# Two transformer layers: when results are taken, where up-projections, the last gate and the relu product stand

## The chip, the cores and the metric

One core of a Trainium2 chip. Its engines are TensorE (matmuls), VectorE, ScalarE, GpSimd and SyncE (it issues the loads); they run unsynchronised and wait for each other on semaphores. The metric is the time of one execution on the device in microseconds; the time before is 3451.94 us, the median of 3 runs (3451.68 to 3452.9).

## The reference, cut to what matters

Everything is fp32. A first model of two layers (FFN, retention or neighbourhood attention, FFN) runs on 512 rows and ends in an RMS norm; its 256 rows feed a second model of two layers, of width 1024, which is all that the change touches apart from bookkeeping. One layer of it:

```python
h = _rms_norm(x, norm_mix_pre[l])
proj = jnp.einsum('bsd,de->bse', h, w_in[l])
dq, dk, dv, mq, mk, mv, c_q, c_kv, k_pe, g = jnp.split(proj, IN_OFFSETS, axis=-1)
oa = _diff_attention(...)                 # 4 heads, two softmaxes each, then a sub-norm
ob = _moba_attention(mq, mk, mv, ...)     # 4 heads; 256 tokens are one block: causal softmax
q = jnp.einsum('bsr,re->bse', _rms_norm(c_q, mla_q_norm[l]), mla_w_uq[l])     # + rope on 32 dims
kv = jnp.einsum('bsr,re->bse', _rms_norm(c_kv, mla_kv_norm[l]), mla_w_ukv[l]) # k: 64 dims + rope(k_pe)
oc = _dense_causal_attention(q, k, v, ...)                                    # 8 heads
br = jnp.einsum('bsgc,gcd->bsgd', stack([oa, ob, oc]), w_branch[l])
gates = jax.nn.sigmoid(g.reshape(B, S, N_BRANCH, D_MODEL))
mixed = jnp.einsum('bsd,de->bse', jnp.sum(gates * br, axis=2), w_out[l])
x = x + _rms_norm(mixed, norm_mix_post[l])
h = _rms_norm(x, norm_mlp_pre[l])
u = jnp.square(jax.nn.relu(jnp.einsum('bsd,df->bsf', h, w_up[l])))            # 1024 -> 4096
x = x + _rms_norm(jnp.einsum('bsf,fd->bsd', u, w_down[l]), norm_mlp_post[l])
```

## The kernel before

**Projections.** All projections go through one list of `Gemm` objects. Each is cut into groups, a group into chunks. A usual group is one weight block of 8 K tiles of 128 by 256 columns, 1 MB, and makes two chunks of 128 output rows by 256 tokens. To keep fp32 accuracy, both operands are held as a high part and a low part in a reduced format, and each product is three matmuls (high-high, high-low, low-high): 24 matmuls a chunk, 48 a group. The branch groups have 4 K tiles, 24 matmuls. The up-projections of the latent attention are one group each: `mla_uq` 8 chunks of 6 matmuls, `mla_ukv` 8 chunks of 3 and two of 3 that are 512 wide.

**Weights.** SyncE loads block after block into six slots. ScalarE copies a block to `w_high` (L808, two pieces, three buffers), VectorE subtracts to get `w_low` (L1215, two pieces). `splits_upto(s + 1)` at the start of a group's step on these two engines splits the block two groups ahead. So each engine's order is: split a later block, then take the results (evict the chunks) of this group.

**Banks.** A chunk goes to PSUM bank n % 4; TensorE waits for chunk n - 4 to be taken. Even and odd chunks have a semaphore each. Each call of `gemm` on ScalarE and VectorE first waits until the last two chunks before it have been taken.

**Order.** TensorE, ScalarE and VectorE each walk the same program as Python generators; a `yield` ends a group. `both` chains several gemms, `alongside` puts groups of projections between the units of an attention. A unit is one softmax of 128 queries: TensorE makes the scores (L1905, plus bias L1906), VectorE the row maximum (L1411, L1412), ScalarE the exponentials (L974), VectorE a diagonal matrix of inverse sums (`dg`, L1421 with L1424 or L1427), TensorE turns the probabilities with it (L1922), ScalarE copies them (`hf`, L955), TensorE multiplies by the values (L1936), ScalarE and VectorE take the output in two parts (L963, L1436). Scores run two units ahead. In `alongside`, a lag of 1 puts ScalarE and VectorE one unit behind TensorE with each group.

**One layer, in TensorE's order.** `mla_c` (latents, first two groups "wide": both blocks, K tile by K tile, four banks), `diff_q`, `diff_k`, `diff_v`, `mla_uq`, rotation of the rope key, `mla_ukv`, rotations and `moba_q`, the differential attention with `moba_k` and `moba_v` beside it, `gate0`, the sub-norm, the block attention, the latent attention with `branch0`, `gate1`, `branch1`, `gate2` (16 groups) beside its 16 units, `branch2`, `mixed`, norm and residual, then four times `up` (4 groups) and `down` (4 groups), norm and residual. In the first layer these stand at: up-projections 2317 to 2343 us, differential attention 2359 to 2418, block attention 2439 to 2465, latent attention 2471 to 2583, branch2 2583 to 2595, mixed to 2631, the four up and down pairs from 2637 to 2843. The second layer follows 587 us later.

**Taking results.** `row_scaled` and `sigmoid` chunks multiply by the row factor of the norm (`rb`; it isn't applied to the inputs). A gate chunk is one VectorE multiply (L1327) and one ScalarE tanh (L920). A `mix` chunk is multiply (L1375), add (L1380), and for the last branch also a ScalarE high part `yh` (L938) and a VectorE low part `yl` (L1386), which `mixed` reads. A `relu2` chunk of `up` is, one after the other: VectorE max with 0 times the row factor `rb2` (L1359), VectorE square (L1362), ScalarE high part (L934), VectorE low part (L1365). `down` reads the eight chunks of `up` as its K tiles.

**Norms.** ScalarE squares the chunks (L821), TensorE sums them with ones (L1763), ScalarE takes the root (L841), VectorE the reciprocal, TensorE spreads it over the partitions (`spread`, L1778). For a "raw" norm ScalarE copies the spread row to `rb` or `rb2` (`row_out`, L869). `opened` and `joined` place these sums between the K tiles of the wide groups.

## Time and profile before

| | us |
|---|---|
| median of 3 runs | 3451.94 |
| lowest, highest | 3451.68, 3452.9 |
| the profiled execution | 3449.64 |
| span of its trace | 3447.9 |
| TensorE busy | 3236.3 (94%) |
| VectorE busy | 1879.9 (55%) |
| ScalarE busy | 1151.5 (33%) |
| mean granted TensorE clock | 0.960 |

The span runs from the first instruction to the last; 1.7 us of the execution lie around it. Matmuls are pipelined and their ends are modelled, so TensorE's 94% is not how full it is; its waits and the starts of its instructions tell more. DMA engines are busy 39% of the time for the weights.

### The profile page before, as it was taken

What the parts mean: (1) busy time and instruction counts of PE and PEld (TensorE: products, weight loads), DVE (VectorE), ACT (ScalarE), POOL (GpSimd) and SP (SyncE); (2) the same over time, 40 slices, a digit from 0 to 9 for tenths busy, and PEclk for the clock granted to TensorE, in tenths of its full rate; (3) what the DMA queues carried; (4) which work ended last, traced back from release to release, by engine and by line L of the source; (5) the groups of instructions that cost most, each with busy time, mean ns of one, the idle gap of its engine ahead of it and who ended that gap; (6) DMA issues with size and microseconds to landing.
All of it is one profiled execution on the core that took longest, in us unless ns stands there. A gap on an engine that the chain in (4) does not pass through costs nothing.

```text
span 3447.9 us, 46967 instructions
## 1 busy us (share of the span) xinstructions
PE 3236.3 (94%) x19181; PEld 2794.8 (81%) x19181; DVE 1879.9 (55%) x3739; ACT 1151.5 (33%) x1945; POOL 38.5 (1%) x74
## 2 busy tenths in 40 slices
PE   8999999999899999999999999998898998888898
PEld 4788878888678888788877779996887998778798
DVE  1777663544468966433344345555456666445665
ACT  2322232323232222322233334442444344344442
POOL 1000000000000000000000000000000000000000
PEclk9999999999999999999989999998999999899899
DMA  8445441221145656323232125652234554224352
GB/s 254 122 146 170 129 141 62 92 68 62 61 123 169 216 171 189 86 80 110 80 100 66 61 81 153 178 176 74 86 103 150 163 167 125 62 86 147 110 183 87
DMA packets 501215, 421.36 MB, mean 122 GB/s; under 512 B 9947, under 2 KB 497675, under 8 KB 501001
## 3 DMA queue, kind: packets, MB, share of 16 engines
q1 hardware_dynamic: 497976, 412.33, 38.9%
q0 software_dynamic: 3024, 6.03, 0.7%
q8 instruction: 152, 2.49, 0.3%
q14 instruction: 63, 0.51, 0.0%
HBM read 417.20 MB, written 1.12 MB: 121 GB/s over the span
## 4 chain that ended last, share of the span: by engine, by line
PE 86%; DVE 9%; ACT 3%; issue 2%; SPq 0%; DMA 0%; DVEq 0%; ACTq 0%
PE gemm L1829 71%; DVE w_low L1215 3%; PE aux L1763 2%; PE aux L1922 2%; PE aux L1905 2%; PE aux L1936 2%; ACT w_high L808 1%; PE aux L1906 1%; PE gemm L1978 1%; PE aux L2067 1%; PE aux L1797 1%; DVE hf L1362 1%; DVE xt L1257 1%; DVE yt L1359 1%; PE aux L2055 1%
## 5 line engine op out<-in xcount | busy, mean ns | idle before, releaser
L1215 DVE TENSOR_TENSOR w_low<-raw,w_high 128x1024 fp32r<-128x1024 f32 (+2 forms) x720 | 759.1, 1096 | 369.8 <-ACT w_high L808 368.7
L808 ACT ACTIVATE w_high<-raw 128x1024 fp32r<-128x1024 f32 (+2 forms) x720 | 647.9, 948 | 692.4 <-PE gemm L1829 408.3
L1829 PE MATMUL gemm<-xh,w_high 128*128 128x512 f32 (+1 forms) x1792 | 676.9, 378 | 21.1 <-DVE xl L1243 21.1
L1829 PE MATMUL gemm<-xl,w_high 128*128 128x512 f32 (+1 forms) x1792 | 667.2, 372 | 0.0
L1829 PE MATMUL gemm<-xh,w_low 128*128 128x512 f32 (+1 forms) x1792 | 666.9, 372 | 0.0
L1829 PE MATMUL gemm<-yh,w_high 128*128 128x256 f32 x1344 | 392.2, 292 | 29.0 <-DVE yl L1386 10.2
L1829 PEld LDWEIGHTS gemm<-xh,w_high 128*128 128x128 f32 x1792 | 342.0, 191 | 93.2 <-issue 18.2
L1829 PEld LDWEIGHTS gemm<-xh,w_low 128*128 128x128 f32 x1792 | 342.2, 191 | 63.1
L1829 PEld LDWEIGHTS gemm<-xl,w_high 128*128 128x128 f32 x1792 | 342.7, 191 | 60.8 <-issue 0.7
L1829 PE MATMUL gemm<-yl,w_high 128*128 128x256 f32 x1344 | 384.5, 286 | 0.0
L1829 PE MATMUL gemm<-yh,w_low 128*128 128x256 f32 x1344 | 383.7, 286 | 0.0
L1186 DVE SCALAR_TENSOR_TENSOR macc<-raw,sc,macc 128x256 f32<-128x256 f32 x728 | 301.9, 479 | 4.0
L1829 PEld LDWEIGHTS gemm<-yh,w_high 128*128 128x128 f32 x1344 | 260.2, 194 | 37.2 <-issue 18.1
L1829 PE MATMUL gemm<-hid_high,w_high 128*128 128x512 f32 (+1 forms) x704 | 262.2, 372 | 0.0
L1829 PEld LDWEIGHTS gemm<-yl,w_high 128*128 128x128 f32 x1344 | 260.5, 194 | 0.1
L1829 PEld LDWEIGHTS gemm<-yh,w_low 128*128 128x128 f32 x1344 | 260.0, 193 | 0.0
L1829 PE MATMUL gemm<-hid_low,w_high 128*128 128x512 f32 (+1 forms) x704 | 259.5, 369 | 0.0
L1829 PE MATMUL gemm<-hid_high,w_low 128*128 128x512 f32 (+1 forms) x704 | 259.1, 368 | 0.0
L1829 PE MATMUL gemm<-act_high,w_high 128*128 128x256 f32 (+1 forms) x752 | 223.7, 298 | 30.9 <-DVE act_low L1365 17.9
L1829 PE MATMUL gemm<-act_low,w_high 128*128 128x256 f32 (+1 forms) x752 | 217.7, 290 | 0.0
L1829 PE MATMUL gemm<-act_high,w_low 128*128 128x256 f32 (+1 forms) x752 | 217.2, 289 | 0.0
L1349 DVE TENSOR_TENSOR hf<-sq,gemm 128x512 f32<-128x512 f32 (+1 forms) x88 | 54.5, 620 | 284.2 <-PE gemm L1829 284.2
(303 smaller groups left out, 4414.1 us busy)
## 6 DMA issues: line engine op xcount, KB each, us to landing
raw<-in_ffn_w_in SPq DMA_DIRECT2D x176, 512.0 KB, 5.3
raw<-in_w_mod SPq DMA_DIRECT2D x72, 1024.0 KB, 7.1
raw<-in_w_in SPq DMA_DIRECT2D x50, 1024.0 KB, 5.2
raw<-in_w_up SPq DMA_DIRECT2D x32, 1024.0 KB, 5.4
raw<-in_w_down SPq DMA_DIRECT2D x32, 1024.0 KB, 5.1
raw<-in_ffn_w_out SPq DMA_DIRECT2D x32, 768.0 KB, 4.6
raw<-in_ret_w_in SPq DMA_DIRECT2D x24, 1024.0 KB, 5.2
raw<-in_ffn_w_out SPq DMA_DIRECT2D x32, 640.0 KB, 4.1
```

The source lines that it names most:

```text
L808: act.activation(wh[i % SPL][:, a:b], raw[slot_of["w", i]][:, a:b], ACT.Copy).then_inc(w_high, 1)
L1186: dve.scalar_tensor_tensor(out=acc, in0=raw[slot][:, WB * k:WB * k + WB], scalar=sc[:, k, v:v + 1], in1=acc, op0=ALU.mult, op1=ALU.add).th ...
L1215: dve.tensor_tensor(wl[slot][:, a:b], raw[slot][:, a:b], wh[i % SPL][:, a:b].bitcast(F32), ALU.subtract).then_inc(w_low, 1)
L1257: dve.scalar_tensor_tensor(out=x_t[:, (N["s0"] + k) % 4, :], in0=N["src"](c)[:, ts * T:ts * T + T], scalar=N["scale"](c, ts), in1=mean_of( ...
L1349: dve.tensor_tensor(hf[:, pr % 2, 0:tok], sa[:, pr % 2, 0:tok], ps[:, 0:tok], ALU.mult).then_inc(odd_free, 1)
L1359: dve.scalar_tensor_tensor(out=yt[:, pr % 4, :], in0=ps[:, 0:T], scalar=0.0, in1=rb_of[name][0], op0=ALU.max, op1=ALU.mult).then_inc(free( ...
L1362: dve.tensor_tensor(hf2[:, pr % 2, :], yt[:, pr % 4, :], yt[:, pr % 4, :], ALU.mult).then_inc(hid_f, 1)
L1763: ins = pe.matmul(mean_of(N)[:, o:o + w], s_q[:, i % N["sqn"], P * j:P * j + P], fsq[:, c, :] if kind == "f" else ones[:, 0:1], start=c == ...
L1829: ins = pe.matmul(out, l_, r_, start=first and j == 0, stop=last and j == 2)
L1905: pe.matmul(sc_[:, 0:k], un["qk"][0], un["qk"][1], start=True, stop=True, skip_group_check=True)
L1922: ins = pe.matmul(aux[2][:, P * kt:P * kt + P], pe_[:, uq % a.slots, P * kt:P * kt + P], dg_[:, uq % a.slots, :], start=q == 0, stop=q == ...
L1936: ins = pe.matmul(aux[3][r0:r1, 0:P], tile["v"](kt), pt_[:, tg % 2, P * kt:P * kt + P], start=kt == 0, stop=kt == nkt - 1)
```

## The change

- `alongside`: lag now counts groups. ScalarE and VectorE split and take a group when TensorE is at the next one, no longer one unit later.
- The values `diff_v` and `moba_v` become two gemms of one group each; `mla_uq` stands between the halves of `diff_v`, `mla_ukv` after the second.
- In groups of 8 or more chunks (`mla_uq`, `mla_ukv`) the split of a later block comes after the sixth chunk instead of before the first.
- The rope: the key is rotated after `mla_ukv`, its seven copies move into the first gate, the angles are made between the two groups of `diff_q`; TensorE waits for less before its rotations.
- The block attention has no group step of ScalarE and VectorE in it; both groups of the gate are taken behind it.
- `gate2` leaves the latent attention. It and `branch2` become four gemms of one group each, in turn: gate quarter, branch quarter. The mixed result goes to `ah`, `al` instead of `yh`, `yl`, and `mixed` is wide.
- `up`: ScalarE makes relu of the chunk, VectorE multiplies it with the chunk itself; high and low part of a chunk come after the next chunk's product. The row factor of this norm is no longer applied: the MLP's output is off by its square per token, and the norm behind it gets eps divided by the fourth power of the factor instead, made of one tiny operation (`joint`) with the mean square.
- The sums of squares of the last two chunks of the first norm move from K tile 7 to K tile 3 of the first projection.

```diff
@@ alongside
-                y = x - lag
-                upto = y * nb // na if not atts[name].narrow else 0 if y < 0 else 1 + y * (nb - 2) // na
-                while done < upto:
+                upto = 1 + x * (nb - 2) // na if atts[name].narrow else x * nb // na
+                while done < upto - lag:
@@ gemms
-            qkv("diff", 0, 0.125, q2, k2, v2)
+            q_and_k("diff", 0, 0.125, q2, k2)
+            v_half("diff", 0, v2, 0)
             add(f"mla_uq{l}", ...
+            v_half("diff", 0, v2, 1)
...
+            for g in range(2):
+                gate(g, f"gate{g}{l}", 0, 4)
+                branch(g, f"branch{g}{l}", 0, 4)
+            for q in range(4):
+                gate(2, f"gate2{l}{q}", q, q + 1)
+                branch(2, f"branch2{l}{q}", q, q + 1)
+            add(f"mixed{l}", "copy_y", A_groups(A["w_out_2"][l], D),
+                (lambda c: ah[:, c, :], lambda c: al[:, c, :]), L, arg=0)
@@ with_mla
-            return [f"{k}{l}" for k in ("branch0", "gate1", "branch1", "gate2")]
+            return [f"{k}{l}" for k in ("branch0", "gate1", "branch1")]
@@ scalar: gemm
-                    splits_upto(s + 1)
+                    if len(ch) < 8:
+                        splits_upto(s + 1)
...
                         elif g.kind == "relu2":
-                            pr = g.hid0 + i
-                            act.wait_ge(hid_f, g.rl0 + i + 1)
-                            act.activation(ah[:, i, :], hf2[:, pr % 2, :], ACT.Copy).then_inc(hid_high, 1)
+                            act.wait_ge(chunk_ready, n + 1)
+                            if i >= 4:
+                                wait_chunk_out(act, n - 4)
+                            act.activation(yt[:, i % 4, :], ps[:, 0:T], ACT.Relu).then_inc(relu_ready, 1)
+                            for k in ([i - 1] if i else []) + ([i] if i == g.nch - 1 else []):
+                                wait_chunk_out(act, g.n0 + k)
+                                act.activation(ah[:, k, :], hf2[:, k % 2, :], ACT.Copy).then_inc(hid_high, 1)
...
                         n += 1
+                        if ci == 5 and len(ch) >= 8:
+                            splits_upto(s + 1)
@@ vector: gemm
-                            dve.scalar_tensor_tensor(out=yt[:, pr % 4, :], in0=ps[:, 0:T], scalar=0.0, in1=rb_of[name][0],
-                                                     op0=ALU.max, op1=ALU.mult).then_inc(free(n), 1)
-                            dve.wait_ge(free(n), n // 2 + 1)
-                            dve.tensor_tensor(hf2[:, pr % 2, :], yt[:, pr % 4, :], yt[:, pr % 4, :],
-                                              ALU.mult).then_inc(hid_f, 1)
-                            dve.wait_ge(hid_high, pr + 1)
-                            dve.tensor_tensor(al[:, i, :], hf2[:, pr % 2, :], ah[:, i, :].bitcast(F32),
-                                              ALU.subtract).then_inc(hid_low, 1)
+                            dve.wait_ge(relu_ready, g.rl0 + i + 1)
...
+                            dve.tensor_tensor(hf2[:, i % 2, :], yt[:, i % 4, :], ps[:, 0:T], ALU.mult).then_inc(free(n), 1)
+                            for k in ([i - 1] if i else []) + ([i] if i == g.nch - 1 else []):
+                                dve.wait_ge(hid_high, g.hid0 + k + 1)
+                                dve.tensor_tensor(al[:, k, :], hf2[:, k % 2, :], ah[:, k, :].bitcast(F32),
+                                                  ALU.subtract).then_inc(hid_low, 1)
@@ vector: inverses
+                if N["name"][:8] == "mlp_post":
+                    dve.wait_ge(sq_used, N["sq0"] + N["nc"])
+                    dve.scalar_tensor_tensor(out=joint[:, 2:4], in0=mean_of(N)[:, 0:2], scalar=1.0 / D, in1=joint[:, 0:2],
+                                             op0=ALU.mult, op1=ALU.add).then_inc(var_ready, 1)
...
+                elif N["name"][:7] == "mlp_pre":
+                    chain(dve.tensor_tensor(joint[:, 2:4], root[:, 0:2], root[:, 0:2], ALU.mult))
+                    dve.scalar_tensor_tensor(out=joint[:, 0:2], in0=joint[:, 2:4], scalar=EPS, in1=joint[:, 2:4],
+                                             op0=ALU.mult, op1=ALU.mult).then_inc(inv_ready, 1)
@@ tensor
-                        spread(norms[pre])
+                        if pre == "mix_pre1":
+                            spread(norms[pre])
...
-                if k == DC - 1:
+                if k == 3:
                     for c in range(6, DC):
                         mean_square(norms["final"], c)
+                if k == DC - 1:
                     spread(norms["final"])
...
-                    pe.wait_ge(roped, 2 * MH * l + (MH + k - 3 if k >= 4 else 1))
+                    if k >= 3:
+                        pe.wait_ge(roped, 2 * MH * l + (1 if k == 3 else k - 2))
...
-                pe.wait_ge(o_low, atts[f"mla{l}"].t1)
-                run(gemm(f"branch2{l}"))
-                run(gemm(f"mixed{l}", lambda kc: pe.wait_ge(mix_low, 8 * l + kc + 1)))
+                for q in range(4):
+                    run(gemm(f"gate2{l}{q}"))
+                    pe.wait_ge(o_low, atts[f"mla{l}"].t1)
+                    run(gemm(f"branch2{l}{q}"))
+                run(gemm(f"mixed{l}", lambda kc: pe.wait_ge(mix_low, 8 * l + kc + 1), wide=True))
```

## Rows read from the trace of the kernel before

**Rows 1.** The page, part 4: shares of the chain that ended last.
```profile
PE 86%; DVE 9%; ACT 3%; issue 2%; SPq 0%; DMA 0%; DVEq 0%; ACTq 0%
```

**Rows 2.** TensorE's waits, 2262 to the end: waited for, us in total, times, longest.
```profile
PE aux L1922 <- DVE dg L1427: 21.0, 7, 4.6
PE gemm L1829 <- DVE act_low L1365: 17.9, 12, 4.0
...
PE aux L1922 <- DVE dg L1424: 11.2, 8, 3.2
PE aux L1922 <- ACT hf L955: 10.9, 6, 3.2
PE gemm L1829 <- DVE yl L1386: 10.2, 5, 4.0
...
PE gemm L1829 <- DVE w_low L1215: 5.9, 2, 3.0
...
PE aux L1778 <- DVE r_columns L1232: 1.7, 1, 1.7
```

**Rows 3.** Windows: us, busy of PE, PEld, DVE, ACT, POOL (count), granted clock, DMA share, GB/s.
```profile
2317.00:2343.00 26.00, 16.97 (x90) 13.47 (x88) 16.00 (x36) 9.67 (x17) 0.00 (x0) 0.80 0.31 93
...
2359.00:2418.00 59.00, 48.26 (x279) 39.19 (x279) 21.50 (x75) 15.72 (x51) 0.00 (x0) 0.86 0.17 54
...
2439.00:2470.00 31.00, 24.56 (x170) 22.42 (x169) 15.10 (x55) 13.08 (x43) 0.00 (x0) 0.94 0.14 44
...
2700.00:2747.00 47.00, 45.82 (x386) 45.52 (x386) 31.48 (x48) 18.98 (x24) 0.00 (x0) 1.00 0.56 180
...
2905.00:2925.00 20.00, 14.70 (x87) 11.40 (x85) 12.67 (x27) 9.19 (x15) 0.00 (x0) 0.90 0.43 127
...
2941.00:3005.00 64.00, 53.61 (x279) 43.50 (x280) 21.42 (x74) 16.16 (x52) 0.00 (x0) 0.76 0.16 50
```

**Rows 4.** Chain of waits, 2471 to 2583 us: start, us, what.
```profile
2481.11 4.44 PE gemm L1829 x24
...
2487.42 3.04 PE gemm L1829 x24
...
2498.20 5.88 PE gemm L1829 x48
...
2534.37 5.03 PE gemm L1829 x24
```

**Rows 5.** Chain of waits, 2316 to 2343 us.
```profile
2321.50 2.00 ACT w_high L808 x2
...
2331.39 1.29 DVE mk L1672 x6
...
2332.71 2.36 DVE w_low L1215 x2
```

**Rows 6.** TensorE's waits, 2359 to 2412 us.
```profile
PE aux L1922 <- DVE dg L1427: 10.7, 4, 4.6
```

**Rows 7.** TensorE's waits, 2470 to 2583 us.
```profile
PE aux L1922 <- DVE dg L1424: 5.6, 4, 3.2
```

**Rows 8.** Chain of waits, 2583 to 2610 us.
```profile
2594.02 1.05 ACT w_high L808
...
2600.38 1.05 ACT w_high L808
```

**Rows 9.** Chain of waits, 2652 to 2680 us.
```profile
2660.96 1.22 DVE w_low L1215
...
2667.26 1.22 DVE w_low L1215
```

**Rows 10.** Groups of instructions from 2150 us: busy us, mean ns, idle before them.
```profile
L1365 DVE TENSOR_TENSOR act_low<-hf,act_high 128x256 fp32r<-128x256 f32 x64 | 27.2, 426 | 31.1 <-ACT act_high L934 31.1
...
L934 ACT ACTIVATE act_high<-hf 128x256 fp32r<-128x256 f32 x64 | 26.7, 418 | 112.5 <-DVE hf L1362 112.5
...
L893 ACT ACT_TABLE_LOAD x3 | 3.8, 1283 | 0.1
```

More of the change, by code:

```diff
@@ L1111, in _ @@
                 run(gemm(f"mla_c{l}"))
[L1112 removed]
+                steps = both(*(gemm(f"diff_{k}{l}") for k in "qk"))
                 next(steps)
@@ L1120, in _ @@
                 highs(N)
-                run(steps)
                 if l == 0:
@@ L1724, in _ @@
                                              op1=ALU.subtract).then_inc(sub_low, 1)
-                steps = attention(f"moba{l}")
-                next(steps)
-                next(steps)
-                next(gate)
-                for x in range(len(atts[f"moba{l}"].units) - 1):
-                    next(steps)
-                run(steps)
+                run(attention(f"moba{l}"))
                 run(gate)
                 alongside(f"mla{l}", attention(f"mla{l}"), gemm, with_mla(l), 1)
-                run(gemm(f"branch2{l}"))
+                for q in range(4):
+                    run(gemm(f"gate2{l}{q}"))
+                    run(gemm(f"branch2{l}{q}"))
                 run(gemm(f"mixed{l}"))
@@ L1873, in gemm @@
                     if gi and name in follows:
-                        mean_square(follows[name], 2 * gi - 2)
-                        mean_square(follows[name], 2 * gi - 1)
+                        for c in range(0 if wide and gi == 2 else 2 * gi - 2, 2 * gi):
+                            mean_square(follows[name], c)
                     n += len(ch)
```

148 lines of the change are left out of this document (83 added, 65 removed).

## The prediction

> **What bounds the kernel now.** I read the page first. Its chain of work that ended last is 86% TensorE, 9% VectorE and 3% ScalarE [rows 1], and TensorE's largest share is one line, the matmuls of all projections. So the time is TensorE's work plus its waits. The change touches only the two layers from 2262 us to the end, so next I read who TensorE waits for there [rows 2]; all of that list is about 135 us. The reader should see which producers stand in it: the diagonals of the attention (21.0 and 11.2 us), the turned probabilities (10.9), the low parts that "down" and "mixed" read (17.9 and 10.2), weight splits that came late (5.9). Nearly all are results of VectorE or ScalarE that were queued behind something else. Third, I read the windows [rows 3]: the MLP of one "up" and one "down" is nearly dense (45.82 of 47.00 us, clock 1.00), while beside the differential attention the granted clock is 0.86 in the first layer and 0.76 in the second. A wait there costs twice: the idle time, and slow matmuls behind it. A run of 24 projection matmuls takes 3.04 us where nothing stalled before it and 4.44 or 5.03 us behind a stall [rows 4].
>
> Lengths given below as from start to start are read between the first matmuls of two stretches in the list of instructions in time. Unit prices: 48 matmuls (a group of 256 columns over 8 K tiles) 5.88 us, 24 matmuls 3.04 us [rows 4]. A full weight block is split in 2 ScalarE pieces of 1.05 us and 2 VectorE pieces of 1.22 us [rows 8, 9]; with the first ScalarE piece ahead, that is about 3.4 us from start to end. One 128x256 operation is 0.42 us on either engine [rows 10].
>
> **Part 1, up-projections between value halves.** The chain of waits from 2316 to 2343 us runs TensorE, ScalarE split (2.00 us, two pieces), then later 6 copies of the rope key (1.29), a VectorE split (2.36), and only then the eviction that frees TensorE's bank [rows 5]. So TensorE, whose up-projection chunks are only 6 or 3 matmuls long, waits for evictions queued behind splits, copies and (first layer only) the angle computation. From the first up-projection matmul (2317.0) to the first of the next projection (2343.3) is 26.2 us in the first layer and 20.6 in the second; TensorE is busy 16.97 of 26 and 14.70 of 20 us there [rows 3]. After the change the evictions of these groups come before the split (it moves behind the sixth chunk), a half of the values (5.88 us, unchanged work) lies between the two, the copies go elsewhere and the angles are made earlier. What is left: 48 matmuls 5.9, 24 matmuls 2.9, six wide ones about 1.5, rotations 2.2, sum 12.5. A new wait appears: rotation 3 still needs the rotated key, and VectorE makes that now behind a split (2.4), two evictions (1.1) and three rope steps (1.3), some of it after TensorE is through: I walk through it to 2.5 us. So about 15 us: **saves 11.3 in the first layer, 5.7 in the second**. Cover: the seven key copies (about 1.5 us) move behind a reciprocal during the first gate, where VectorE has slack before its next eviction; without that cover they cost 1.5 each layer.
>
> **Part 2, a whole group later beside attention.** In the differential attention TensorE puts a group in at three places. ScalarE and VectorE take the group one unit later, so the next diagonal is queued behind a split and an eviction, while TensorE has nothing left to do. It waits 10.7 us there in the first layer, 4.6 at the longest, twice [rows 6]. With the lag of a group, these engines do that work while TensorE is in the next group (3.4+0.7 us under 5.88). Each of the two waits falls to some 0.3 us: 9 us a layer. On top, the matmuls behind the stalls ran slowly; I take back 1 us in the first layer and 3 in the second. In the block attention the same wait is one of 3.2 us, listed as waiting for the turned probabilities [rows 2]: 3.2. In the latent attention the waits for diagonals are 5.6 us [rows 7], another 2.0 for turned probabilities, and two 24-runs behind them lost 1.4 and 2.0 us [rows 4]. There four gate groups go away (their 23.5 us of work moves to part 3), 12 groups are spread over 16 units, and six units have no group. I give back about 4.5 us: a 24-run (3.04) that must cover a full split plus eviction (4.1) leaves 1.3, the same at the end 0.9, and six bare units at 0.3. The gate's first block is split one step before TensorE wants it, with 1.1 us to wait. Net 6.7. **Sum of part 2: 20 us in the first layer, 22 in the second.** Attention waits for o_low of the last tile are covered by the first quarter of the gate.
>
> **Part 3, last gate and branch in turn, mixed wide.** Before, the last branch is 8 chunks in a row; per two chunks ScalarE and VectorE need a split and twice (multiply, add, ScalarE copy, subtract), one after the other. The chain from 2594.02 to 2600.38 is such a period, 6.36 us with full blocks [rows 8], against 3.04 of TensorE. So "mixed" starts late and stutters: over both layers TensorE waits 10.2 us for low parts and 5.9 for blocks [rows 2], 11.5 a layer from start to start, slow matmuls included. Now a quarter is 5.88+3.04-0.3 = 8.6 us of TensorE, and for the other two engines: full split 3.4, two gate evictions and a tanh 1.2, small split 1.5, two chunks of 1.76: 9.3 us by hand. They fall behind by 0.8 a quarter; the last quarter must also split two full blocks of "mixed". The wide "mixed" needs both blocks and all four banks, so it starts only about 7 us after the branch's last matmul, and slowly. 11.5 against 10: **saves 1.4 a layer**. This is the edit with the least in it.
>
> **Part 4, relu product at once, row factor folded away.** At the end of "up" the low parts come late. The period of a group in the chain is 6.30 us (2660.96 to 2667.26) [rows 9], above TensorE's 5.88, since VectorE has three operations of 0.42 per chunk and waits for ScalarE in between (31.1 us in 64 chunks, 0.49 each [rows 10]). After: VectorE two, ScalarE two, and the low part of a chunk is taken after the next product, so no engine waits for the other. Per group: split 2.4 + 4x0.42 = 4.1 us of VectorE. "Up" becomes TensorE's own. The waits of "down" (17.9 us for both layers [rows 2]) go. In each of three later stages that is 1.36 us from start to start, 4.1 a layer. In the first stage the row factor goes too: the spread, its copy on ScalarE (0.39) and the wait for them; TensorE then starts its third group 1.4 us earlier, and the two late groups and the start of "down" (the 4.0 us wait of [rows 2] is one of three there) go: from 2652.8 to 2700.3 is 47.5 us, after it 0.8+1.3+11.5+22.9 = 36.5. **Saves 15 a layer.** The factor comes back as one tiny VectorE operation before the root of the MLP's last norm: 0.25 us each layer, lost. Relu on ScalarE is in no row. Its price lies between that of a copy of this shape (0.418) and a table load of 1.283 at every change between it and the copy [rows 10]; the nearest row is the copy, which I take. One load per stage would be 8x1.3 = 10 us, which I keep for the range.
>
> The Trainium skill, page "ScalarE: Activation LUTs", section "Rules for kernel authors", speaks against this edit: relu and products belong on VectorE. By rows the two engines cost the same at this shape in fp32, and in the MLP's window VectorE is the fuller one (31.48 against 18.98 of 47 us [rows 3]). The same page, "Table sets: the hidden batching unit", has relu in every set, which would make the loads zero; no row here shows it.
>
> **Part 5, first norm.** The mean squares of the last two chunks move from the last row of the first projection to its fourth; the roots run beside the matmuls. The wait of 1.7 us for them [rows 2] goes, 1.9 from start to start: **1.9**, once.
>
> **The sum.** First layer 11.3+20+1.4+15+1.9-0.25 = 49.4; second 5.7+22+1.4+15-0.25 = 43.9; together 93 less 1 us for small things, 92. The profiled execution has a span of 3447.9 us and took 3449.64 in all, 2.3 below the median 3451.94. The new span is 3356, in all 3358, and as a median **3360 us**.
>
> **Rivals.**
> (A) *The engines stay tied, and the gain is half in the attention stages.* In the latent attention the groups are thinner, and diagonals could wait for splits just as before: part 2's 6.7 there is gone, the differential part gives 5 less, and the quarter chain of 9.3 against 8.6 costs 5 more in part 3. 2x(6.7+5+5) = 33 less: 3393. For it: 9.3 is above 8.6, and several 24-runs are too short a cover. Against: 4.1 us fits under 5.88.
> (B) *More than forecast*, because the clock stays up once the stalls are gone: in the second layer the differential stretch is at 0.76 for 64 us [rows 3]; at 0.95 it would be some 8 us shorter, and similar small gains elsewhere: 3338.
> (C) *Slower than before*: the clock falls in the latent attention and the turn behind it. Place: the 12 groups (45 us) and 16 units, now with six units that have no dense group. Price: the 5.03 us run of 24 against 3.04 [rows 4], about 0.65 of a group's time more, up to 0.8 when all is slow: 45x0.8 = 36, and 16 for the attention's own matmuls; 52 a layer, 104 in all, against 93 saved: 3463. It decides once some nine tenths of that stretch run at the lower level. For it: 0.76 beside the differential attention. Against: that is behind 5 us stalls, and the block attention without groups has 0.94 [rows 3].
> (D) *The change does not do what it says*: the lag delays the split of the next block as well, and TensorE waits for weights instead of diagonals, once per group. 2 us for 15 groups a layer gives back 60: 3420. Against: I find each block split one group before its use.
>
> On (C), the Trainium skill, page "TensorE: Matmul & The Clock Gate", section "What's actually happening", says that the slow level is the default and activity releases it. By that rule, sparser stretches would move towards the 3463 of (C), and removed stalls towards (B); the trace agrees as far as the runs behind stalls go.
>
> **Chances.** Forecast (3342 to 3377) 0.62; A 0.20; B 0.08; C 0.03; D 0.05, a tail of A and D that ends near the old time 0.02. From no change one can tell about 0.2% (7 us). Faster 0.95, same 0.02, slower 0.03. The range takes in A's value and B's: 3338 to 3395; the likeliest case alone is 3342 to 3377, where the table loads (+10) and the uncertain clock (plus or minus 8) lie.
>
> **What would show it.** Right: no wait for the low parts in "down"; the waits for diagonals under 8 us instead of 32 in two layers; the first stage of the MLP near 36 us from its last mean square; the up-projection stretch without its value half near 15 us; one wait of about 7 us before "mixed", for a low weight or a product of the last branch. Wrong: waits of TensorE for the low weights inside the attention stages (D), clock under 0.8 from the latent attention to "mixed" (C), table loads among the relus. What would make the number wrong most easily is part 3, worked out, and the clock.

## The result

The changed kernel takes 3342.87 us (median of 4 runs, 3341.46 to 3343.44), the kernel before took 3451.81 in the runs beside it (3446.8 to 3452.9). The ratio is 0.9687, with a 95% interval from 0.967 to 0.9703: 109 us less, where 92 were forecast. The profiled span fell from 3447.9 to 3341.6 us, and the granted clock over the whole span rose from 0.960 to 0.974.

The page of the changed kernel, parts 1 and 2 (busy time; TensorE's clock in 40 slices):

```profile
PE 3191.3 (96%) x19173; PEld 2760.6 (83%) x19173; DVE 1849.5 (55%) x3679; ACT 1166.9 (35%) x2007; POOL 38.5 (1%) x74
...
PEclk9999999999989999999998999999999999999899
```

TensorE does the same matmuls, but for 8 tiny ones, in 45 us less busy time (3236.3 before), at a higher granted clock, so I count those 45 us as clock. The other 61 us of the 106 are time in which it stood idle.

The chain of the changed kernel cannot be set beside [rows 1], since the profile could follow it through a small part of the span only. TensorE's waits from 2262 us to the end can (columns as in [rows 2]):

```profile
PE gemm L1866 <- DVE yt L1411: 17.2, 4, 7.3
...
PE aux L2174 <- DVE mk L1706: 4.5, 2, 2.3
PE aux L1959 <- DVE dg L1465: 4.2, 8, 1.3
...
PE gemm L1866 <- DVE hf L1398: 2.7, 2, 1.3
...
PE aux L1959 <- ACT hf L988: 2.2, 8, 0.4
...
PE aux L1959 <- DVE dg L1462: 0.7, 2, 0.3
```

The 21.0 and 11.2 us for diagonals of [rows 2] are 4.2 and 0.7, the 10.9 for turned probabilities are 2.2, and the 17.9 for the low parts that "down" reads are gone. Around the last branch 17.2 us are waited, of which 7.3 is one wait ahead of "mixed" in each layer; this is no less than the 10.2 for low parts and 5.9 for blocks that stood there in [rows 2]. New are 4.5 us for a rotated key.

Windows of the two differential attentions, of the latent attention, of the gate and branch quarters in turn, and of "mixed" in the first and the second layer (columns as in [rows 3]):

```profile
2346.00:2391.00 45.00, 42.80 (x277) 34.48 (x278) 21.38 (x74) 15.18 (x51) 0.00 (x0) 1.00 0.24 71
2882.00:2927.00 45.00, 42.80 (x277) 34.36 (x277) 21.62 (x75) 15.17 (x51) 0.00 (x0) 1.00 0.23 71
2441.00:2516.00 75.00, 67.12 (x512) 61.21 (x510) 43.38 (x123) 32.20 (x91) 0.00 (x0) 1.00 0.36 112
...
2521.00:2564.00 43.00, 34.84 (x289) 34.53 (x290) 31.25 (x56) 18.79 (x32) 0.00 (x0) 0.95 0.60 195
2564.00:2595.00 31.00, 28.23 (x228) 27.96 (x227) 14.93 (x24) 13.71 (x23) 0.00 (x0) 0.94 0.42 137
...
3099.00:3133.00 34.00, 30.19 (x228) 29.84 (x228) 16.16 (x27) 13.86 (x23) 0.00 (x0) 0.85 0.38 124
```

Against [rows 3] the differential attention takes the same matmuls in 42.80 us of TensorE, where it took 48.26 in the first layer and 53.61 in the second, and its clock is 1.00 where it was 0.86 and 0.76.

Where the time went, from start to start of the same matmuls in the lists of instructions in time (both layers together, us saved; a group that moved from one stretch to another is taken out of both at its own 5.6 or 23.4 us; the first row counts from the start of the span and holds 0.8 us by which the changed kernel comes later to the two layers):

| stretch | forecast | measured |
|---|---|---|
| first norm and projections ahead | 1.9 | 3.2 |
| up-projections (part 1) | 17.0 | 16.1, less 2.1 given back in the next projection |
| differential attention (part 2) | 22 | 13.8 + 18.8 = 32.6 |
| block attention (part 2) | 6.4 | 8.2 |
| latent attention (part 2) | 13.4 | 15.3 |
| last gate and branch, mixed (part 3) | 2.8 | 3.9 |
| MLP (part 4, with the 0.5 lost) | 29.5 | 29.2 |
| sum | 93 | 106.3 |

### The profile page after: what moved, and what is told of

Its sections match the earlier page's. It is cut to its first block and busy times, and to the rows that moved or that the text cites. A ratio compares the mean times of both kernels' runs of the same rounds, so it can differ in the third digit from the quotient of the medians.

```text
span 3341.6 us, 47023 instructions
## 1 busy us (share of the span) xinstructions
PE 3191.3 (96%) x19173; PEld 2760.6 (83%) x19173; DVE 1849.5 (55%) x3679; ACT 1166.9 (35%) x2007; POOL 38.5 (1%) x74
## 5 line engine op out<-in xcount | busy, mean ns | idle before, releaser
L1866 PE MATMUL gemm<-yh,w_high 128*128 128x256 f32 x1216 | 353.1, 290 | 16.6 <-DVE yl L1306 7.1
L1866 PE MATMUL gemm<-yl,w_high 128*128 128x256 f32 x1216 | 347.3, 286 | 0.0
L1866 PE MATMUL gemm<-yh,w_low 128*128 128x256 f32 x1216 | 346.9, 285 | 0.0
L1866 PE MATMUL gemm<-act_high,w_high 128*128 128x256 f32 (+1 forms) x880 | 252.0, 286 | 14.5 <-DVE yt L1411 14.5
L1866 PEld LDWEIGHTS gemm<-yh,w_high 128*128 128x128 f32 x1216 | 234.8, 193 | 22.2 <-issue 17.2
L1866 PE MATMUL gemm<-act_low,w_high 128*128 128x256 f32 (+1 forms) x880 | 249.0, 283 | 0.0
L1866 PE MATMUL gemm<-act_high,w_low 128*128 128x256 f32 (+1 forms) x880 | 248.8, 283 | 0.0
L1866 PEld LDWEIGHTS gemm<-yl,w_high 128*128 128x128 f32 x1216 | 235.0, 193 | 0.1
L1866 PEld LDWEIGHTS gemm<-yh,w_low 128*128 128x128 f32 x1216 | 234.7, 193 | 0.0
```

Of the source, the lines that this page charges most:

```text
L1866: ins = pe.matmul(out, l_, r_, start=first and j == 0, stop=last and j == 2)
```

## The experiments

Each run is the changed kernel with one or two edits. The changed kernel's own median is 3342.87; the medians of the kernel before beside the sets of runs were 3451.8 to 3453.6, so the sets can be compared within about 2 us.

### The lag taken back

```diff
-                upto = 1 + x * (nb - 2) // na if atts[name].narrow else x * nb // na
-                while done < upto - lag:
+                y = x - lag
+                upto = y * nb // na if not atts[name].narrow else 0 if y < 0 else 1 + y * (nb - 2) // na
+                while done < upto:
```

> The changed kernel with one edit taken back: beside attention the grouped results trail by one unit again, not by a whole group. Theory (the lag itself brings what both attentions gained): the wait of TensorE for the accumulators that VectorE frees behind the diagonal sums comes back in both layers, the stretch from the first to the third unit of the difference attention goes from 38.2 us back to about 52 in the first layer and 57 in the second, the latent attention loses about 7 per layer, and the kernel takes about 3385 to 3395 us (+42 to +52). Of that I expect some 20 us in idle waits and the rest as slower matmuls, granted clock back under 0.9 in that stretch. Rival (the clock of 1.00 in that stretch comes from the denser work ahead of it, not from the stalls inside it): the waits return, 18 to 20 us and no more, the clock stays at 1.00, and the kernel takes about 3363.

Measured: 3428.26 us, ratio 0.9926 (0.9911 to 0.9941). The lag is worth 85 us, twice what I expected, and four fifths of the whole change. Windows of this run (differential attention of layer one and two, latent attention of layer one), then TensorE's waits in them:

```profile
2346.00:2406.00 60.00, 49.15 (x285) 40.20 (x285) 21.27 (x74) 16.46 (x53) 0.00 (x0) 0.86 0.17 53
2922.00:2986.00 64.00, 53.29 (x293) 43.08 (x292) 22.61 (x76) 16.66 (x53) 0.00 (x0) 0.81 0.17 50
2455.00:2558.00 103.00, 80.07 (x515) 72.82 (x514) 43.34 (x123) 32.52 (x91) 0.00 (x0) 0.85 0.26 82
```

```profile
PE aux L1960 <- DVE dg L1466: 10.8, 5, 4.6
...
PE aux L1960 <- DVE dg L1463: 12.8, 5, 3.9
PE aux L1960 <- ACT hf L989: 5.5, 2, 3.5
```

The differential attention is that of the kernel before again: the two long waits, and a clock of 0.86 and 0.81. From its first group to its third it takes 52.3 and 55.1 us, against 38.2 in both layers of the changed kernel. All that stands ahead of it is as in the changed kernel, so the clock fell behind the stalls inside. The rival, that the work ahead held the clock up, is out. But that is 31 us in both layers. The other 53 are in the latent attention, where I had put 14: in the first layer TensorE waits 18.3 us there for diagonals and turned probabilities where the changed kernel waits 0.9, and the clock is 0.85, not 1.00.

### The gate back beside the latent attention, with either lag

```diff
-            return [f"{k}{l}" for k in ("branch0", "gate1", "branch1")]
+            return [f"{k}{l}" for k in ("branch0", "gate1", "branch1", "gate2")]
...
                 for q in range(4):
-                    run(gemm(f"gate2{l}{q}"))
                     run(gemm(f"branch2{l}{q}"))
```

> The changed kernel with the third gate back beside the latent attention (16 groups there again, one for each of its 16 units) and the last branch as four quarters in a row behind it; the lag of a whole group stays, and the product of the three branches stays wide. It sizes the turn by itself, with the lag given. Theory (the turn is worth little, 2.7 us a layer from start to start, and its groups would be covered beside attention just as well once the lag is there): 3343 to 3350 us, so 0 to 7 above the changed kernel. Rival (the gate between the branch's quarters is the cover for the product's low parts, which come back as waits of 5 to 6 us a layer, and slow matmuls behind them): 3355 to 3365.

> The same kernel, third gate beside the latent attention, and the lag of one unit as well: with these two edits taken back the order beside both attentions is that of the kernel before. The run with the lag alone taken back lost 85 us where I had expected 42 to 52; my explanation now is that the lag of a unit and the thinner groups hurt each other: with 16 groups over 16 units, a lag of one unit is a lag of one group in nearly every unit, with 12 groups it is none in the units that have no group. Theory (this interaction): here the lag costs only what the difference attention gives, 14 us in the first layer and 19 in the second, and a few us at the two units of the latent attention that have no group; 3378 to 3392 us, and TensorE's waits for diagonals come to about 30 us, not 47 and 12 more for turned probabilities. Rival (the lag by itself costs those 85 us wherever the gate stands): 3425 or more.

Measured: 3350.79 us with the lag of a group, 3395.98 with the lag of a unit. The four corners, as medians:

| | gate in turn (12 groups beside) | gate beside (16 groups) |
|---|---|---|
| lag of a group | 3342.9 | 3350.8 |
| lag of a unit | 3428.3 | 3396.0 |

So the lag brings 45 us with 16 groups and 85 with 12. The theory of an interaction holds (waits for diagonals 32.7 us in all, about 30 expected), and its time (3378 to 3392) was too low by 4 us: the latent attention gave 8.9 and 7.3 us besides the 31 of the differential one, the last part again by clock, 0.95 against 1.00. Windows of that attention, first layer, lag of a unit and of a group, and the waits with the lag of a unit:

```profile
2456.00:2561.00 105.00, 92.20 (x680) 85.62 (x678) 56.93 (x143) 41.15 (x103) 0.00 (x0) 0.95 0.35 110
```

```profile
2442.00:2539.00 97.00, 88.32 (x685) 81.92 (x685) 57.26 (x143) 40.87 (x104) 0.00 (x0) 1.00 0.39 120
```

```profile
PE aux L1956 <- DVE dg L1460: 5.6, 4, 3.2
PE aux L1970 <- issue: 5.2, 11, 0.7
PE aux L1956 <- ACT hf L987: 2.0, 1, 2.0
```

The 5.6 and 2.0 are those of the kernel before [rows 7]. The reason is in the line of the diff. With 16 groups over 16 units TensorE puts in a group at nearly every unit, so "one unit later" and "one group later" are the same thing but for two units. With 12 groups some units have none. At such a unit a lag of one unit gives ScalarE and VectorE the last group's split and evictions ahead of the next diagonal, while TensorE has nothing but the diagonal to go on with. The thinner the groups, the more such units. The list of TensorE's instructions bears this out: with the lag of a unit, its waits over 1.5 us in this attention are six (1.7 to 3.9 us) with 12 groups, where six units have no group, and two (3.2 and 2.0 us) with 16, where two have none; each stands at such a unit. Taking the gate out alone would have lost 32 us; with the lag it wins 8. Of these 8 us, 3.2 in the first layer and 4.1 in the second lie from the latent attention to the end of "mixed". The wait ahead of "mixed" shows the turn's cover, here without it:

```profile
PE gemm L1862 <- DVE yt L1408: 11.4, 1, 11.4
```

It is 7.3 us with the turn. Of the two expectations on the turn the smaller one is the nearer; the measured time lies 0.8 us above its range.

### The gate's group inside the block attention

```diff
-                run(attention(f"moba{l}"))
+                steps = attention(f"moba{l}")
+                next(steps)
+                next(steps)
+                next(gate)
+                run(steps)
```

> The changed kernel with one hunk taken back on ScalarE and VectorE: they take the gate's third group inside the block attention, behind its second step, as before, where now they take it behind the whole attention. Theory (the 4.06 us that the block attention gained in the first layer are this hunk, since the run with the unit lag left them untouched): one wait of 3 to 3.5 us for turned probabilities returns in each layer, +6 to +8.5 in all, 3349 to 3352. Rival (they came from what stands ahead of it, such as the key copies and the clock): within 1.5 us of 3343.

Measured: 3350.47 us, +7.6. TensorE's waits in the block attention, from 2412 us, of this run:

```profile
PE aux L1967 <- ACT hf L988: 3.4, 2, 3.2
```

In the changed kernel this row is 0.5 us. The stretch between its two groups is 25.07 and 25.01 us here, 20.95 and 20.94 in the changed kernel, and 25.01 and 25.07 before. This hunk is the whole gain of the block attention; the lag has no part in it.

### The up-projections: one order, the other, and both

Both value halves ahead:

```diff
                 run(gemm(f"diff_v{l}0"))
+                run(gemm(f"diff_v{l}1"))
                 run(gemm(f"mla_uq{l}"))
-                run(gemm(f"diff_v{l}1"))
                 run(gemm(f"mla_ukv{l}"))
```

> The changed kernel with one move taken back: both halves of the difference attention's values ahead of the two up-projections, none between them; the weight split behind the sixth chunk, the early angles and the key copies at the gate stay. Theory (the half between the two gives ScalarE and VectorE the time for splits and evictions of the up-projections): TensorE waits 2 to 4 us a layer more between the two up-projections, and the kernel takes 3347 to 3352 us. Rival (the late split alone had freed the evictions, and the half between does nothing): within 1.5 us of 3343.

Split ahead of the evictions:

```diff
-                    if len(ch) < 8:
+                    if len(ch) < 8 or name[:5] == "mla_u":
                         splits_upto(s + 1)
...
-                        if ci == 5 and len(ch) >= 8:
+                        if ci == 5 and len(ch) >= 8 and name[:5] != "mla_u":
```

> The changed kernel with one order taken back, in the two up-projections alone: the next weight block is split ahead of the six or more evictions of a group, as before, not behind the sixth of them; the half of the values stays between the two, the early angles too. The run with both halves together had shown that the half between them is worth about 1 us. Theory (it is the late split that freed TensorE there, most of the 10.8 us of the first layer): TensorE waits again for evictions behind splits, about 2.5 us at each of the up-projections, and slow matmuls follow; 5 to 8 us a layer, 3353 to 3358. Rival (the first layer gained mainly by the early angles and by the key copies that went to the gate, and the half between the values covers the split wherever it stands): 3343 to 3347.

Both edits together:

> The changed kernel with both orders of the up-projections taken back together: the two halves of the values ahead of them, and the next block's split ahead of the evictions. Each of these alone had cost 1 us. What stays of the change there is that the angles come early, that the seven key copies went to the gate, and that VectorE rotates the key behind the second up-projection. Theory (the half between and the late split cover the same split, so that either is enough and the loss appears only when both are gone): +3 to +5 us a layer, 3349 to 3353, with waits of TensorE for evictions in both up-projections. Rival (the splits were never the trouble; the angles, the copies and the rotation, 4.1 and 1.5 and 1.7 us of VectorE in the way in the kernel before, were all of it): within 2 us of 3343.

Measured: 3343.99, 3344.02 and 3343.25 us. All three are within 1.2 us of the changed kernel, and the rival is right each time. (The last expectation says that each alone had cost 1 us; against its own runs of the kernel before, the ratios 0.9690 and 0.9686 do not tell that from nothing.) TensorE's waits from 2308 to 2346 us with both taken back, then in the changed kernel:

```profile
PE gemm L1866 <- DVE mk L1372: 1.0, 1, 1.0
PE aux L2174 <- DVE mk L1706: 0.8, 1, 0.8
PE gemm L1866 <- ACT mk L941: 0.7, 1, 0.7
PE gemm L1866 <- DVE mq L1372: 0.7, 1, 0.7
PE gemm L1866 <- ACT mq L941: 0.2, 1, 0.2
```

```profile
PE aux L2174 <- DVE mk L1706: 2.3, 1, 2.3
```

And of the kernel before, 2312 to 2358 us:

```profile
PE gemm L1829 <- ACT mq L914: 3.8, 1, 3.8
PE gemm L1829 <- DVE mk L1332: 3.5, 1, 3.5
PE aux L2133 <- DVE mv L1332: 1.0, 1, 1.0
PE gemm L1829 <- ACT mk L914: 0.7, 1, 0.7
```

With both orders as before, five small waits of 3.4 us in all stand where one of 2.3 stands in the changed kernel, and TensorE's slow 48 matmuls behind them take 7.2 us instead of 8.2. From start to start of part 1's stretch (its value half taken out) it is 17.1 us with both taken back and 15.4 in the changed kernel, in each layer, against 26.2 and 20.6 before; the faster matmuls behind give 1.05 and 0.7 of the 1.7 back. The kernel before has 9.0 us of waits in the first layer. So most of the gain of part 1 comes from what left the way. Of the 9.0, 1.0 is the wait for `mv`: TensorE no longer waits for the end of `mla_ukv` before its rotations. For the rest: in the kernel before, VectorE makes the angles from 2317.76 to 2320.7 us in the first layer and ScalarE follows until 2321.5, ahead of the first eviction of the queries; and between the two up-projections, from 2329.05 to 2332.7 us, VectorE ends the angles, rotates the key and makes its seven copies. The half between the up-projections and the late split are worth nothing that can be told from the medians, and at most 1.7 us a layer in the stretch itself. Which of the moves (angles, key copies, key rotation, TensorE's own wait) brings how much was not run apart; that the second layer, which has no angles, gained 5.3 us against 10.8 speaks for about half by the angles in the first.

### The relu product as before

```diff
-                            dve.wait_ge(relu_ready, g.rl0 + i + 1)
+                            dve.wait_ge(chunk_ready, n + 1)
...
-                            dve.tensor_tensor(hf2[:, i % 2, :], yt[:, i % 4, :], ps[:, 0:T], ALU.mult).then_inc(free(n), 1)
...
+                            dve.tensor_scalar(yt[:, i % 4, :], ps[:, 0:T], 0.0, None, ALU.max).then_inc(free(n), 1)
+                            dve.wait_ge(free(n), n // 2 + 1)
+                            dve.tensor_tensor(hf2[:, i % 2, :], yt[:, i % 4, :], yt[:, i % 4, :],
+                                              ALU.mult).then_inc(relu_ready, 1)
```

(With it, each chunk is rounded and its low part taken right behind the square, as before, and VectorE waits once a stage for the readers of its buffer.)

> The changed kernel with the relu product as before: VectorE takes the maximum out of the accumulator, squares it, ScalarE rounds, VectorE takes the low part of the same chunk, all in a row; the row factor stays where the change put it. Theory (the chain max, square, round, difference of one chunk paces the 64 chunks, and the order of the change takes it apart): the first stage of a layer goes from 54.65 us back to about 62 and the pair of stages loses 13 to 14 per layer, so the kernel takes about 3369 to 3372 us (+26 to +29), and what is left of the prediction's 15 per layer is the folded row factor with 1.5 to 2. Rival (most of the gain is from the row factor and the operands that come earlier through it): +5 us per layer or less, 3353 or below.

Measured: 3370.66 us, +27.8, as expected. The row of [rows 2] is back to the tenth:

```profile
PE gemm L1866 <- DVE act_low L1401: 17.9, 12, 4.0
```

From the last mean square to the end of the first "down" it is 47.5 us in the kernel before, 46.2 here and 38.0 in the changed kernel: the folded row factor gives 1.2, the order and the relu's place on ScalarE together 8.3. ScalarE's rows from 2262 us to the end of the changed kernel:

```profile
...
L965 ACT ACTIVATE act_high<-hf 128x256 fp32r<-128x256 f32 x64 | 26.3, 411 | 5.9 <-DVE hf L1398 5.9
L962 ACT ACTIVATE yt<-gemm 128x256 f32<-128x256 f32 x64 | 24.1, 380 | 63.3 <-PE gemm L1866 63.3
...
L1007 ACT ACT_TABLE_LOAD x2 | 2.6, 1283 | 0.0
```

The relu takes 380 ns, less than the copy's 411. The nine table loads of this stretch stand at other lines (two of them in the row shown); none stands at the relu's line or at the copy's.

### Two steps further

Low parts of the sum behind both products of a quarter:

```diff
-                            if g.arg == 2:
-                                dve.wait_ge(mix_f, m + 1)
-                                dve.wait_ge(mix_high, 8 * (m // 16) + i + 1)
+                            if g.arg == 2 and ci == len(ch) - 1:
+                                for b in range(len(ch)):
+                                    j = i - len(ch) + 1 + b
+                                    dve.wait_ge(mix_f, m - i + j + 1)
+                                    dve.wait_ge(mix_high, 8 * (m // 16) + j + 1)
...
```

> The changed kernel with one order changed: in the last branch VectorE makes both products and sums of a quarter first and takes both low parts behind them, where now it takes each low part right behind its own sum and so waits for ScalarE's rounding each time. Theory (the last quarters are paced by VectorE and ScalarE handing one value back and forth, 9.52 us a quarter against 8.6 of TensorE): the quarter falls to about 8.6, the wait ahead of the product of the three branches falls from 7.3 us (sum of both layers) to about 3, and the kernel takes 3334 to 3337 us. Rival (the waits hang on ScalarE's two operand splits of a quarter, which this order does not touch): the quarter stays at 9.5 and the time within 1.5 us of 3343.

Measured: 3337.17 us, at the upper end of what was expected; the span is 6.9 us below that of the changed kernel. All quarters now follow each other on TensorE after 8.5 to 8.6 us, its own time, where the last one of the changed kernel came after 9.5. The wait ahead of "mixed" falls from 7.3 to 4.4:

```profile
PE gemm L1867 <- DVE yt L1411: 11.4, 4, 4.4
```

The 7.3 and the 4.4 are one wait in one layer each. The expectation had read 7.3 as the sum of both layers, which is 14.5; the wait fell by less than it says.

The key rotated inside its up-projection, ahead of the late split:

```diff
                         if ci == 5 and len(ch) >= 8:
+                            if name[:7] == "mla_ukv":
+                                rope(int(name[7]), MH)
                             splits_upto(s + 1)
...
-                rope(l, MH)
```

> The changed kernel with one move: VectorE rotates the latent key inside the up-projection of keys and values, after its sixth chunk, where now it does it behind the last one, as the first of five rotations. Theory (TensorE's wait of 2.65 us in the first layer and 2 in the second for the rotation's buffer is this late rotation, and the 1.05 us lost behind it are matmuls at the low clock after that wait): the wait goes or halves, the 48 matmuls behind it take about 6 us instead of 8.2, and the kernel takes 3334 to 3338 us. Rival (VectorE has the same five rotations to do, only the next of them is waited for): the wait moves to another rotation, the low part's split in the up-projection comes later by the 2 us of the rotation, and the time is within 1.5 us of 3343 or up to 4 us above.

Measured: 3337.11 us; the span is 7.4 us shorter. Both sides were half right. The wait for the rotated key is gone and the 48 matmuls behind it take 5.66 us instead of 8.23. (The 2.65 us of the expectation is from start to start of two rotation matmuls; the wait itself is 2.3.) A wait for a later rotation comes up behind the next projections:

```profile
PE aux L1943 <- DVE mq L1708: 3.7, 2, 1.9
```

The span fell by 3.7 us a layer, the wait alone by 0.4. Most of what it buys is that a projection runs at the high clock: behind the new wait of 1.9 us the granted clock does not fall, it is 1.00 from 2320 to 2390 us and from 2856 to 2925.

Both together, and then with "mixed" narrow:

> The changed kernel with the two improvements that each gained about 6 us in single runs: the low parts of the three branches' sum behind both products of a quarter, and the latent key rotated inside its up-projection. Theory (they stand at two places with independent waits, 5.7 and 5.8 us by medians, 6.9 and 7.4 by the profiled spans): 3330 to 3332 us by the median, span about 3327. Rival (they share a cause, so that only one of the gains is there): 3337.

> The version with both improvements (low parts behind both products, key rotated early; 3329.5) and the product of the three branches narrow instead of wide: 16 groups of two chunks, so that it starts with one split block and two banks free, where the wide form needs two blocks and all four banks. Theory (with the turn, the wait of 4.4 us ahead of it is for the last low parts and the banks, and the narrow form needs the same low parts at its first group): within 2 us of 3329.5 to either side. Rival (the wide form's larger start is what is waited for): 3322 to 3326. Other rival (narrow groups of 2.8 us are shorter than the split of their block and stutter as before the change): 3335 or more.

Measured: 3329.45 us (ratio 0.9650, 0.9636 to 0.9663) and 3328.89 us (0.9645, 0.9632 to 0.9658). The first is 0.6 us below what was expected. The two gains add up: 13.4 us below the changed kernel, 122 below the kernel before. Wide or narrow makes no difference that can be measured, as the first theory had it. In the first layer the narrow form starts its first 18 matmuls without a wait, and then waits for the low parts of the last quarter (2540 to 2580 us):

```profile
PE gemm L1868 <- DVE act_low L1423: 3.3, 2, 2.9
```

## Why the prediction was right, and where not

**Faster, and the size.** 3342.87 us lies in the range of 3338 to 3395. It lies 17 us under the forecast, 0.9 us inside the lower end of the likeliest case (3342 to 3377) and 5 us above the value of rival (B), which is what happened in the attention: the clock stayed up once the stalls were gone. Of the 17 us, 14 are saved work and waits (106.3 of span against 92). The rest is the step from span to median: 4 us had been added, since the profiled run before lay 2.3 below its median, and for the changed kernel it is 1.3.

**The term that was mis-sized** is "on top, the matmuls behind the stalls ran slowly; I take back 1 us in the first layer and 3 in the second". The waits fell as worked out, from 10.7 us [rows 6] to 2.1, which is 8.6 against the 9 forecast. The matmuls gave 5.2 us in the first layer and 10.2 in the second (13.8 and 18.8 less 8.6 each). The windows had the number ready: 48.26 and 53.61 us of busy TensorE [rows 3] for matmuls that take 42.80 at the full clock. I had priced the slow level by single runs of 24 matmuls and not by the busy time of the stretch.

**Part 2** was right about the mechanism in the differential attention, which the run with the unit lag confirms. In the block attention it was right by size (3.2 a layer against 4.1) and wrong by cause: it is the gate's group that moved behind the attention, a hunk of its own, so the near number is luck. In the latent attention the net of 6.7 a layer was near (7.6 and 7.7; the terms listed there add up to 6.5 to 7.0), but I had priced the lag and the move of the gate side by side. They can't be: the move loses 32 us without the lag and wins 8 with it.

**Part 1** was right by size, 11.3 and 5.7 forecast against 10.8 and 5.3, and mostly wrong by cause. The step that failed is "after the change the evictions of these groups come before the split, a half of the values lies between the two": both taken back cost 0.4 us by the medians and 1.7 a layer in the stretch itself. The angles and copies, named in passing ("the copies go elsewhere and the angles are made earlier"), carried most of it, with TensorE's own shorter wait before the rotations. The sum came out because it went by TensorE's work alone, 12.5 us, and all but one of the waits did go, whatever removed them; as to the cause, that is luck. The wait of 2.5 us for the rotated key came as foretold (2.3). What was missing is its price behind: the next 48 matmuls took 8.2 us and not 5.7, and the projection lost 1.05 us a layer against before.

**Part 3** was right: 2.7 and 1.2 us from start to start against 1.4, a wait of 7.3 against "only about 7 us". What it leaves out is the clock behind that wait: the 144 matmuls that follow take 18.7 us in the first layer and 20.0 in the second (clock 0.94 and 0.85 in the windows above), where 144 in a row at the full clock take 17.1 in the kernel before. That is why the second layer gained less. The reason given for the wait, two full splits and four banks, is only a part of it: 2.9 of the 7.3 go when VectorE no longer waits for ScalarE after each sum, and of the 4.4 that stay, the narrow form still waits 3.3 for the last low parts. The terms given for a quarter on VectorE and ScalarE (3.4, 1.2, 1.5 and two of 1.76) add up to 9.6, not 9.3; measured, the second and the third quarter start 8.6 and 8.5 us after the one ahead, which is TensorE's own time, and the fourth after 9.5, with a wait of 0.8 in it.

**Part 4** was right: 13.6 and 15.7 against 15. Table loads (+10 in the range) did not come. The wait for low parts in "down" is gone. Its first stage took 38.0 us in the first layer and 36.7 in the second, against 36.5 forecast; in both TensorE waits 1.3 us for the first two products, and in the first the 96 matmuls behind it take 13.1 us instead of 11.6. No run changes the order alone or the engine of the relu alone.

**Part 5** was right in kind and too small: the wait of 1.7 us is gone, the two spreads there take 1.0 us less, and the 96 matmuls behind them 11.6 us instead of 13.2. From its first matmul to the up-projections, the moved half of the values taken out, the first layer gained 4.3 us against 1.9; the second, where nothing was forecast, lost 0.6. No run takes this edit back alone.

**The rivals.** (A) and (D) asked for waits for diagonals, or for weights, inside the attention; the first sum to 4.9 us, of the second there is none. (C) asked for a clock under 0.8 from the latent attention on. It is 1.00 in that attention, with six units that have no dense group, 0.95 in the quarters behind it, and 0.94 and 0.85 in the two windows of "mixed", behind the wait of 7.3 us. On the rule quoted there, the page "TensorE: Matmul & The Clock Gate" of the Trainium skill, section "What's actually happening", the trace agrees for the stalls: it is waits, not thinner work, that brought the clock down in these stages (in the latent attention 1.00 with 12 groups, waits of at most 0.7 us and the lag of a group; 0.85 with the same 12 groups, waits up to 3.9 us and the lag of a unit).

On the rule of the Trainium skill, page "ScalarE: Activation LUTs", section "Rules for kernel authors", that relu belongs on VectorE (the reason given there is the speed in bf16), the measurement differs in effect: the run with relu on VectorE, all in fp32, is 27.8 us slower. It has the old order too, so how much of that is the engine alone stays open. What the same page of the Trainium skill has in its section "Table sets: the hidden batching unit", relu in every set, agrees with the trace: 64 relus between 64 copies, and no table load at either line.

## What to carry to other kernels

Where a clock falls behind stalls, price a stall by the busy time of its whole stretch against the busy time of the same matmuls where nothing stalls, and not by its idle time. Set how far a helper engine trails by the groups that the leading engine puts in, not by steps that may hold none: the same edit that spreads groups thinner can cost 32 us or win 8, depending on that. And before the named edit gets the gain, look at what else left the queue in the same stretch; only taking the edit back alone tells.

## What the runs showed of the hardware

- A short wait made a long run slow. In the changed kernel one wait of 2.3 us is followed by 48 matmuls in 8.23 us instead of 5.66. With both orders of the up-projections taken back, five waits of at most 1.0 us stand ahead, and the same 48 matmuls take 7.19. In the run with the early rotation no wait stands there and they take 5.66. The length of the waits does not order these times: in the kernel before, 9.0 us of waits stand ahead, 3.8 the longest, and the same 48 matmuls take 7.17.
- In the latent attention of the changed kernel TensorE is busy 67.12 of 75 us, with gaps up to 0.7 us, and the granted clock is 1.00. In the unit-lag run it is busy 80.07 of 103 us with gaps up to 3.9 us, for the same matmuls, at 0.85.
- ScalarE's relu from the accumulator at 128x256 takes 380 ns, its copy of the same shape from `hf` to the high part 411 ns, and going from one to the other costs no table load.
